# One of nine modulation groups moves from TensorE in the first FFN to VectorE in the gated unit, one step ahead of each gate

## The reference

```
mx = (silu(c)     @ mod_w[i] + mod_b[i]).reshape(9, 1024)     # latent tokens
mc = (silu(c_ctx) @ mod_w[i] + mod_b[i]).reshape(9, 1024)     # context tokens
x  = x + 0.5 * mx[2] * swiglu(rms_norm(x, g0) * (1 + mx[1]) + mx[0])
x  = x + mx[5] * mixer(rms_norm(x, g1) * (1 + mx[4]) + mx[3])
x  = x + 0.5 * mx[8] * swiglu(rms_norm(x, g2) * (1 + mx[7]) + mx[6])
# the S5 mixer ends in: p = gelu(y) @ glu_w + glu_b;  p[:, :1024] * sigmoid(p[:, 1024:])
```

## Time and profile before

| | |
|---|---|
| time, median of 3 | 2092.8 us (2092.4 to 2093.47) |
| the profiled execution | 2093.45 us, its span 2091.6 us (1.85 us lie outside the span) |
| busy share | TensorE 94%, VectorE 70%, ScalarE 34%, GpSimd 20% |
| granted TensorE clock, mean | 0.978 |
| `f0p2a` and `f0p2b` | about 348 to 470 us from the span's start |
| `glu`, blocks 1 to 7 | 584.2 to 660.7 us |
| `f1p0a` | about 672 to 764 us |
| a `modw` load of 1,024 KB | 5.0 us from issue to landing (median of 66; 4.7 to 11.2) |
| the `cb` load of 1,024 KB | 5.0 us from issue to landing |
| the half-block loads of `glu` (512 KB) | 4.4 us |

### The profile page before, as it was taken

How to read it: one execution, slowest core, us unless ns; L and a number is a source line. 1 busy time by engine, 2 the same in 40 slices (tenths; PEclk the granted TensorE clock), 3 DMA queues, 4 the chain that set the end, 5 groups by cost and what they waited for, 6 DMA issues and landing times.

```text
span 2091.6 us, 37808 instructions
## 1 busy us (share of the span) xinstructions
PE 1968.2 (94%) x15026; PEld 1673.9 (80%) x15026; DVE 1458.7 (70%) x2353; ACT 710.6 (34%) x1138; POOL 421.9 (20%) x356
## 2 busy tenths in 40 slices
PE   5999999998998999999899999998999999879997
PEld 2778778777976788888678888886888988779997
DVE  7968778767645976858898586357677777655555
ACT  4222222223344322222242222225555555426332
POOL 0220110134722220202512021150000000022113
PEclk9999999998999999999999999998999999999999
DMA  8465665557633454544535453222011111015553
GB/s 330 161 243 200 207 222 203 199 167 290 236 121 121 160 176 146 186 136 156 185 121 181 141 188 113 96 86 85 29 45 52 42 43 62 23 61 169 180 177 97
DMA packets 85634, 305.06 MB, mean 146 GB/s; under 512 B 9856, under 2 KB 21632, under 8 KB 76032
## 3 DMA queue, kind: packets, MB, share of 16 engines
q1 hardware_dynamic: 80896, 285.41, 39.7%
q0 software_dynamic: 2304, 9.44, 1.1%
q10 hardware_dynamic: 2304, 8.39, 1.0%
HBM read 275.94 MB, written 27.26 MB: 145 GB/s over the span
## 4 chain that ended last, share of the span: by engine, by line
PE 82%; DVE 8%; ACT 3%; issue 2%; POOL 2%; DMA 2%; DVEq 1%; SPq 0%; ACTq 0%; POOLq 0%
PE PS L230 40%; PE PS L221 6%; PE PS L223 6%; PE PS L222 6%; PE PS L1722 6%; PE PS L1709 6%; DVE wlo L266 2%; PE PS L1306 1%; PE PS L684 1%; DMA et<-in_mod_w 1%; PE PS L1138 1%; DMA raw<-in_w_f0p0a 1%; POOL hidl L651 1%; PE PS L1112 1%; PE PS L1920 1%
## 5 line engine op out<-in xcount | busy, mean ns | idle before, releaser
L266 DVE TENSOR_TENSOR wlo<-raw,whi 128x1024 fp32r<-128x1024 f32 x314 | 451.2, 1477 | 83.7 <-ACT whi L260 81.9
L230 PE MATMUL PS<-hh,whi 128*128 128x512 f32 (+1 forms) x1536 | 443.3, 370 | 19.8 <-DVE hl L451 12.5
L230 PE MATMUL PS<-hl,whi 128*128 128x512 f32 (+1 forms) x1536 | 439.1, 367 | 0.0
L230 PE MATMUL PS<-hh,wlo 128*128 128x512 f32 (+1 forms) x1536 | 438.7, 367 | 0.0
L260 ACT ACTIVATE whi<-raw 128x1024 fp32r<-128x1024 f32 x300 | 301.2, 1052 | 276.9 <-PE PS L223 246.0
L230 PEld LDWEIGHTS PS<-hh,whi 128*128 128x128 f32 x1536 | 277.6, 191 | 73.5 <-issue 16.8
L230 PEld LDWEIGHTS PS<-hl,whi 128*128 128x128 f32 x1536 | 280.0, 191 | 47.1
L230 PEld LDWEIGHTS PS<-hh,wlo 128*128 128x128 f32 x1536 | 279.7, 191 | 47.1
L221 PE MATMUL PS<-hidh,whi 128*128 128x512 f32 (+1 forms) x704 | 257.9, 366 | 11.0 <-POOL hidl L651 8.3
L649 POOL CAST hidh<-gt 128x512 f32 (+2 forms) x88 | 63.0, 716 | 974.0 <-DVE gt L597 974.0
L222 PE MATMUL PS<-hidl,whi 128*128 128x512 f32 (+1 forms) x704 | 255.4, 363 | 0.0
(11 more groups left out here) (344 smaller groups left out, 2597.9 us busy)
## 6 DMA issues: line engine op xcount, KB each, us to landing
modw<-in_mod_w SPq DMA_DIRECT2D x66, 1024.0 KB, 5.0
raw<-in_w_gdn SPq DMA_DIRECT2D x32, 512.0 KB, 3.9
cxd<-cx POOLq DMA_DIRECT2D x16, 576.0 KB, 7.2
cxS<-cxd SPq DMA_DIRECT2D x8, 1152.0 KB, 6.0
raw<-in_w_f0p0a SPq DMA_DIRECT2D x16, 512.0 KB, 7.5
vwd<-vws ACTq DMA_DIRECT2D x16, 512.0 KB, 6.6
raw<-in_w_f0p1a SPq DMA_DIRECT2D x16, 512.0 KB, 5.6
raw<-in_w_glu SPq DMA_DIRECT2D x16, 512.0 KB, 4.4
```

What stands on the lines that cost most here:

```text
L230: ended = pe.matmul(dst, of[:, slot, c:c + P], moving, start=first and part_ == 0, stop=last and part_ == 2)
L266: dve.tensor_tensor(wlo[:, s, c], raw[:, s, c], whi[:, s, c].bitcast(F32), ALU.subtract)\
```

## The change

Group 3 leaves TensorE: `PE_GROUPS` becomes 3, and `f0p2a` and `f0p2b` hold no steps of a group. Its eight steps go to VectorE in the GLU, step k in front of gate k. `cb` is loaded and passed through Silu ahead of the GLU. SP loads each step's 1 MB ahead of a block's weights. The phases of FFN 0 stay written out, and VectorE's GLU loop becomes written out. The rows of `mod_w` for the group are laid out for VectorE on the host. The diff, cut to its core:

```diff
-MODS_IN = {(0, 0): 1, (0, 1): 2, (0, 2): 3, (1, 0): 4, (1, 1): 5, (1, 2): 6, (2, 0): 7, (2, 1): 8}
+MODS_IN = {(0, 0): 1, (0, 1): 2, (1, 0): 4, (1, 1): 5, (1, 2): 6, (2, 0): 7, (2, 1): 8}
-PE_GROUPS = 4
+PE_GROUPS = 3
@@ ffn_act
-                if (f, p) == (1, 0):
-                    act.wait_ge(cb_in, 16)
-                    act.activation(cb[:, :, :], cb[:, :, :], ACT.Silu).then_inc(cb_ready, 1)
@@ s5_sp
             sp.wait_ge(H_ready, NB5)
             load_block(sp, "glu", 1)
+            sp.dma_start(cb[:, :, :], A["cb"]).then_inc(cb_in, 16)
+            sp.wait_ge(Y_ready, NB5)
             sp.wait_ge(turned_twice, 2 * KT)
@@ s5_dve, glu
                 dt = 2 * i + s
+                mods_dve(dve, PE_GROUPS, dt)
                 dve.wait_ge(sig_ready[s], i + 1)
...
-            blocks(dve, "glu", split_lo, glu)
+            blocks(dve, "glu", split_lo, glu, True)
@@ s5_act
             gelu(KT // 2 - 1)
+
+            act.wait_ge(cb_in, 16)
+            act.activation(cb[:, :, :], cb[:, :, :], ACT.Silu).then_inc(cb_ready, 1)
@@ load_both
-                    if name == "f1p0a" and j == 2:
-                        for q in range(2):
-                            sp.wait_ge(x_ready[q], 1 + X_BEFORE[2])
-                        sp.dma_start(cb[:, :, :], A["cb"]).then_inc(cb_in, 16)
@@ sync, glu
-                    load_blocks(sp, name, 1)
+                    for j in range(2, KT):
+                        load_mods(PE_GROUPS, j - 2)
+                        load_block(sp, name, j)
+                    for k in range(KT - 2, KT):
+                        load_mods(PE_GROUPS, k)
@@ sync, f0p2a and f0p2b
+                elif name[:4] == "f0p2":
+                    for j in range(COUNT[name]):
+                        load_block(sp, name, j)
+                        tables_sp(sp, BASE[name] + j)
```

More of the change, by code:

```diff
@@ L548, in down @@
                             tables_pe(pe, BASE[b] + 2 * i + s)
-                loop(pe, n // 2, g, up)
+                loop(pe, n // 2, g or f == 0, up)
                 for s in range(2):
                     pe.wait_ge(hid_ready[s], pairs + n // 2)
-                loop(pe, KT // 4, g, down)
+                loop(pe, KT // 4, g or f == 0, down)
         def ffn_act(act, f):
@@ L576, in after_split @@
                         tables_act(act, BASE[b] + 2 * i + s)
-                blocks(act, a, split_hi, silu, g)
+                blocks(act, a, split_hi, silu, g or f == 0)
                 if g and hosts == KT:
                     mods_rows(act, g, 7)
-                blocks(act, b, split_hi, after_split, g)
+                blocks(act, b, split_hi, after_split, g or f == 0)
         def ffn_dve(dve, f):
@@ L615, in update @@
                         tables_dve(dve, BASE[b] + 2 * i + s)
-                blocks(dve, a, split_lo, gate, g)
+                blocks(dve, a, split_lo, gate, g or f == 0)
                 if p == 0 and not g:
                     dve.wait_ge(mods_ready, mods_done(layer, n_, 2))
-                blocks(dve, b, split_lo, update, g)
+                blocks(dve, b, split_lo, update, g or f == 0)
         def add_to_x(dve, layer, n, dt, c0, bank, order):
```

## The result

The kernel after takes 2098.2 us (median of 8 runs, 2095.1 to 2100.02) beside 2092.81 us for the kernel before (8 runs, 2089.85 to 2096.69). The ratio is 1.0023 with a 95% interval of 1.0012 to 1.0034: 4.8 us slower, 2.5 to 7.1. My forecast was 2095.1 in a range of 2089 to 2100. The median lies in the range. The likeliest case was a time within 0.2% of the kernel before, and the measured 0.23% lies just outside it, on the slow side. The profiled execution of after took 2095.1 us, its span 2093.0.

What follows compares the result with a forecast made beforehand. TensorE was taken to bound the kernel, with VectorE's list taking over in the GLU. First FFN -7.8, f1p0a -2.3, norm's start +12.1 gave +2.0 us: 2095.1 us, range 2089 to 2100.

Steps and rivals of the forecast that it cites:

- What VectorE has to do in the GLU: GLU, first wlo to gate 7: VectorE's list takes 76.6 us plus 11.2 from GpSimd, 87.8, 9.1 more than TensorE's.
- The step of 0.77 and 0.97 us for what GpSimd costs: GLU: each GpSimd square costs VectorE 0.77 us and each addition 0.97, 11.2 us for 7 squares and 6 additions.
- The gate's wait for itself: VectorE's GLU gates: written out, the wait for the gate's own result falls from 0.25 to 0.07 us, 1.3 off.
- Rivals 1: GLU: GpSimd stretches VectorE by under 5.0 us, so TensorE sets the norm's start; 2086.1 us, chance 0.13.
- Rival 2: GLU: each GpSimd instruction blocks VectorE for its whole length, 15.0 us instead of 11.2; 2099 us, chance 0.19.
- What goes in ahead of the GLU: Ahead of block 1's split, ScalarE's table load and Silu of cb add 1.28 + 1.92 = 3.20 us to the chain.
- The sum to the norm's start: End of the GLU: gate 7 starts 12.3 us later, its update is 0.2 shorter, so the norm starts 12.1 later.
- The whole gap goes: 687.42 - 685.08 = 2.34 us: Start of f1p0a: without the Silu, TensorE's gap between blocks 0 and 1 vanishes, giving back 2.34 us.
- I take 7.8: First FFN, f0p2a and f0p2b: removing the group's matmuls gives back 7.8 us, within bounds of 5 and 7.9.
- Rival 3: First FFN gives only 5 us, or cb or a step's load lands late in the GLU; 2098 and up, chance 0.08.

Runs made afterwards that it cites:

- e2: Kernel after with GpSimd's squares and additions ahead of the second FFN's norm cut to 8 of 512 columns; ratio 0.9996 of before.
- e3: Kernel before with only the load and Silu of cb moved ahead of the GLU, group 3 still on TensorE; ratio 1.0020 of before.
- e5: Kernel after with ScalarE's list in f1p0a written out instead of looped; ratio 1.0027 of before.
- e1: Kernel after with group 3's products on VectorE cut from 1024 to 8 columns, loads and waits kept; ratio 0.9995 of before.
- e6: Kernel after with the Silu of cb behind ScalarE's split of block 1 and ScalarE's GLU list written out; ratio 1.0020 of before.
- e7: Kernel after with three constant matmuls ahead of f0p2b's wait, ScalarE's f1p0a and GLU lists written out, Silu behind block 1's split; ratio 0.9991 of before.
- e8: Kernel before with only cb's load and Silu moved behind the GLU's block 1 split, ScalarE's GLU and f1p0a lists written out; ratio 0.9984 of before.
- e9: e7 plus ScalarE making the norm's squares of tiles 0 to 6 and TensorE summing them, GpSimd idle in the GLU; 2086.99 us, 0.9974 of before.

## Why the prediction was nearly right

- **What VectorE has to do in the GLU: right.** 87.8 us predicted, 87.14 measured. The step of 0.77 and 0.97 us for what GpSimd costs held (1.74 for a cycle, 1.72 measured, by after against e2). The gate's wait for itself vanished in the written-out list nearly whole (0.04 us between gate and update), where I took off 0.18 of 0.25. Rivals 1 (under 5.0 us of stretching) and 2 (from 13.4) are out: the list less my 76.6 leaves 10.5, and a little more since the gates were shorter. Added up over the trace, the products are 9.4 us longer than 1.28 each and the splits 1.7 us longer than 1.22, 11.1 in all. Rival 2's reason for the shorter hold-ups, that VectorE's start and end overlap them, no run tests. TensorE was done 7.8 us ahead of gate 7 (some 9 predicted).
- **What goes in ahead of the GLU: right.** 3.20 predicted, 3.22 measured. The first split starts 0.01 us behind its table load. TensorE's cold start, 1.6 us in e3, was not in my sum; in after the list is VectorE's, and it stayed hidden.
- **The sum to the norm's start: right.** From the last Gelu, +12.1 predicted; 3.22 + 8.42 - 0.22 = +11.4 measured.
- **"The whole gap goes: 687.42 - 685.08 = 2.34 us": wrong, and the main failure.** Measured +0.07. TensorE's start of block 1 came 1.4 us sooner, and 1.5 were lost at the phase's end. I had counted the table load that Silu needs only "ahead of the first gate". The Silu had also set the state in which the loop began, and with it gone, two loads went into each pass, the first of them ahead of the split. e5 shows it: with the list written out, the 2.35 us are there.
- **"I take 7.8" for the first FFN: mis-sized in the profiled execution, right in others.** 5.5 in after and 5.3 in e1, where the clock fell; 7.2 to 7.6 in e2, e5 and e6. Rival 3 named 5 us, but for another cause (VectorE's list).
- **The total.** With 11.4 and 0.1 for the GLU and `f1p0a`, and 5.5 to 7.6 for the first FFN, the change costs 3.9 to 6.0 us; 4.8 was measured. My 2.0 lacked 2.4 us in `f1p0a` and up to 2.3 in the first FFN, and had 0.7 too many in the GLU. By its time this is rival 3's case (+4.8 and above, 2098 and up), to which I gave 0.08, but neither of its causes carries it: the first FFN gave 5.5 us or more, and no load came late in after. That 2098.2 lies in the range is in part luck: the range reached to 2100 for the sake of rivals 2 and 3, and the term that failed was in none of them. The low end of the range was a little off too: 6 us of stretching gives 2089.9, not 2089.

What stays open is e5 and e6: their medians lie 3.9 and 2.7 us above their sums. Their intervals (2.5 to 8.6 and 1.7 to 6.7 us above before) leave out the sums of 1.7 and, narrowly, 1.5. Since e7 holds both edits and came where its sum was, I take it for scatter, but that isn't shown.

## What to carry to other kernels

An activation does two things, its own work and the choice of a table, and the table matters to whatever follows it, above all to a loop. Who moves one must ask which table the next loop now starts in. Before a list of products goes to an engine with idle time, add up that engine's whole list from the instant that releases it to its last gate: an engine that sets off level with TensorE ends late by everything that another engine takes from it. And the tail counts, since TensorE was done 7.8 us ahead of gate 7, though the cycle was only 0.5 us too long.

## What the runs showed of the hardware

The granted clock behind a stretch in which TensorE has little to do falls in some executions and not in others. The end of `f1p2b`, where TensorE waits for VectorE's last step, is the same code in all twelve kernels. In before its stretch ran at 1.00, in after at 0.57, and each matmul took 0.43 us instead of 0.23 (first the windows of before, then those of after; then from after's chain):

```profile
1037.00:1041.00 4.00, 2.90 (x13) 2.06 (x11) 3.25 (x5) 0.09 (x1) 3.65 (x3) 1.00 0.89 332
```

```profile
1041.00:1045.00 4.00, 4.00 (x12) 3.14 (x11) 2.57 (x3) 0.00 (x0) 3.65 (x3) 0.57 0.85 331
```

```profile
1042.33 0.43 PE PS L223
1042.75 0.43 PE PS L221
```

From the first update of `f1p0b` to VectorE's reciprocal of the root behind that stretch, six profiles show 274.06 to 274.10 us (before, e1, e3, e7, e8, e9) and the other six 275.39 to 275.47: two values 1.3 us apart. In each of the six longer ones the granted clock fell to the lower of its two levels (1.2 GHz) in that stretch, and in none of the six shorter ones. The executions of one kernel spread by 4.9 us (after, 8 runs) to 11.7 us (before, 35 runs). Such falls, 1.3 us here and 1.9 us in `f0p2b`, can be parts of that, and the DeltaNet's 449.7 to 462.2 us a larger one. So a single profile can mistake such a part for the change's.
